# A seventh parked weight slot in five pieces, merged routing products, and conv taps loaded ahead of weight slots

## The chip, the cores and the metric

The kernel runs on one core of one Trainium2 chip. The metric is the device time of one launch in microseconds (us), the median over the runs shown. The core has five engines with queues of their own: TensorE (PE: matmuls; its weight loads are listed as PEld), VectorE (DVE), ScalarE (ACT), GpSimd (POOL) and SyncE (SP, which only issues transfers here). Transfers of all queues share 16 DMA engines. All data are float32.

## What is computed

One layer of a decoder over 288 tokens: 256 of a prompt, and 32 of eight samples. The first half mixes tokens in two branches, the second is a mixture of experts. Cut to what matters:

```python
def layer(x, conv_buf, ...):
    mix, new_buf, v_rows = token_mixers(rmsnorm(x, norm_mix_g), ...)
    x = x + mix
    x = x + moe(rmsnorm(x, norm_ffn_g), ...)

def token_mixers(h, ...):
    u_a, v_a, c_val, c_gate, g_a, g_b = split(h @ w_in)          # w_in: 1024 x 6144
    y_a = (gelu(u_a) * chunk_spatial_mix(layernorm(gelu(v_a)))) @ w_branch_a
    conv = depthwise_conv(concat(conv_buf, c_val * sigmoid(c_gate)), conv_w)   # 31 taps
    y_b = silu(layernorm(conv)) @ w_branch_b + b_branch_b
    merged = sigmoid(g_a + b_gate_a) * y_a + sigmoid(g_b + b_gate_b) * y_b
    return merged @ w_out, new_buf, v_a

def moe(h, ...):                  # 32 experts, each token goes to its best 4
    logits = h @ w_router + b_router
    gates = softmax(top_4(logits))
    # for each expert e, over the tokens x that chose it:
    #   gate, up = split(x @ w_up[e] + b_up[e]);  act = (clip(up) + 1) * gate * sigmoid(1.702 * gate)
    #   y += gates * (act @ w_down[e] + b_down[e])        w_up[e]: 1024 x 2048, w_down[e]: 1024 x 1024
```

The weights of one expert are 12 MB (1 MB is 1,048,576 bytes here): 8 MB of w_up, 4 MB of w_down.

## The kernel before

**The ring.** All large weights go through `ring`, 12 slots of 1 MB (128 partitions of 8 KB). The mixing half fills it three times with 36 blocks (`load_block`, L346). 32 of them are 256 columns of a weight matrix, which lie in the slot as eight runs of 1 KB on each partition; the four of w_out are runs of 4 KB. In the expert half slots 0 to 7 hold w_up of one expert and slots 8 to 11 its w_down, and every partition gets one run of 8 KB (`load_slot`, L383).

**Parked slots.** While expert e is in the ring, the first six slots of w_up of the next expert are loaded into buffers that the mixing half no longer needs (`parked`, L197: two in `big`, one each in R1, R2, R4 and R3). Each of the R buffers has 2304 columns, of which a slot takes 2048. GpSimd copies a parked slot into the ring in four copies of 512 columns (L530) once it has landed (`parked_full`) and the ring slot has been read for the last time (`released`). Slots 6 and 7 of w_up are loaded into the ring directly.

**SyncE's order** is what paces the transfers, since SyncE waits in order. For each of the 30 experts in the loop of L435 it does this: `release_parked` waits for the use of slots 0 to 5 by the last item of the expert before; `load_up_rest` waits for slots 6 and 7 and loads them; `load_parked_again` loads parked slots 0 and 1 of the next expert, once they have been copied out; `load_down` waits for each of the four w_down slots of the expert before, and loads it; then parked slots 2 to 5 follow. The waits are on `up_used` and `down_used`, which TensorE counts up.

**Items.** An expert is worked on in items of 32 tokens; here there are 52 items for 32 experts. TensorE's loop body (from L1428) does the w_up products of the next item (`up`, L1371, eight slots) between the w_down products of the present one (`down`, L1381, four slots), after gathering, turning and combining rows. Experts are put in an order by their counts, computed in the kernel (L962 to L983), with those of one and of two items spread over the list.

**Start.** SyncE loads x, then weight blocks 0 to 3, then the conv cache, the conv taps (`cw_rows`, 31 partitions), b_up and w_spatial, then blocks 4 to 7 (L353 to L367). TensorE works on blocks 0 and 1 first, then turns cache, taps, b_up and w_spatial (L1086, called from L1184 to L1203), and only then blocks 2 and 3. The convolution on VectorE (L800, 240 instructions) needs all of these.

**Mixing.** TensorE does 32 projections of 8 matmuls each in `kind` 0 to 3 (v, u, gate a, gate b); ScalarE evacuates each, with four PSUM banks in turn: projection n waits for the evacuation of n - 4. At projection 18 (`kind` 2, `c` 2) ScalarE also takes the roots of the variances of v, for which it waits on VectorE (`v_stats`, L599).

**Routing.** After the mixing TensorE counts ranks of tokens and counts of experts with products by triangular matrices and by ones (L1338 to L1353). `keep_busy(n)` (L1104) issues n matmuls of 32 columns whose result nobody reads. SyncE loads the w_down slots of the first expert as w_out has been used (L432), and the sixth parked slot behind them, and then waits for `before_known` (L434).

The lines that set the order around the change:

```python
            for k in range(PARKED - 1):
                load_parked(1, k)
            for k in range(UP_SLOTS, SLOTS):
                sp.wait_ge(*mix_block_used(MIX_BLOCKS - SLOTS + k))
                load_slot(0, k)
            load_parked(1, PARKED - 1)
...
                release_parked(before)
                load_up_rest(here, before)
                load_parked_again(place + 1, after, range(0, 2))
                load_down(here, before)
                load_parked_again(place + 1, after, range(2, PARKED))
```

## Time and profile before

| | |
|---|---|
| median of 3 runs | 1298.35 us (1297.46 to 1301.08) |
| the profiled execution's own time | 1300.47 us |
| its span, first to last instruction | 1298.5 us |
| mean granted TensorE clock | 0.97 |
| PE busy | 1182.5 us, 91% of the span |
| PEld busy | 583.8 us, 45% |
| DVE busy | 605.0 us, 47% |
| POOL busy | 467.2 us, 36% |
| ACT busy | 249.5 us, 19% |
| moved by DMA | 448.97 MB (millions of bytes), mean 346 GB/s |

The shares are means over the whole span, and matmuls are pipelined, so a busy PE is not PE at its peak. The stages have different limits: the mixing half and the routing take the first 341 us or so, the experts the rest. The time of the profiled execution differs from its span by 1.97 us, which lie outside the first and the last instruction.

### The profile page before, as it was taken

The page shows a single profiled execution, that of the slowest core. Times are in us where ns is not written, and L with a number is a line of the kernel's source. Part 1 is how long each engine was busy: PE and PEld are TensorE (multiplying, and loading weights), DVE is VectorE, ACT ScalarE, POOL GpSimd, SP SyncE. Part 2 cuts the span into 40 slices and gives each one's busy share as a digit, 9 for nine tenths or more (in the row PEclk, how much of TensorE's full clock was granted, in tenths as well). Part 3 has the DMA queues.
Part 4 walks back from the last instruction along what each step waited for, and adds up shares of the span by engine and source line. Part 5 has one row for each costly group of instructions (what it writes and reads, how often), then busy time and mean ns, then how long its engine had stood idle before and what let it go on. Part 6 is the DMA issues. An engine that isn't in the chain of part 4 may idle for free.

```text
span 1298.5 us, 30625 instructions
## 1 busy us (share of the span) xinstructions
PE 1182.5 (91%) x11129; PEld 583.8 (45%) x11130; DVE 605.0 (47%) x1256; ACT 249.5 (19%) x487; POOL 467.2 (36%) x833
## 2 busy tenths in 40 slices
PE   8999999999999899899778998989989799899876
PEld 6777777775544233333233442333433233333232
DVE  2999984121444344444342444443534244344243
ACT  2012124001122122122121221221211122122112
POOL 1012300000444444435452445454544444535452
PEclk9999999999799999999999999999999999999997
DMA  9983433244699999999999699999999999999996
GB/s 260 339 260 106 142 118 134 100 142 184 244 391 390 422 421 420 422 421 421 421 421 421 252 405 420 422 421 421 422 420 421 421 421 422 421 421 422 421 421 253
DMA packets 94570, 448.97 MB, mean 346 GB/s; under 512 B 8526, under 2 KB 42894, under 8 KB 45339
## 3 DMA queue, kind: packets, MB, share of 16 engines
q1 hardware_dynamic: 93742, 446.55, 85.8%
q10 hardware_dynamic: 749, 1.19, 0.3%
q0 software_dynamic: 48, 0.85, 0.2%
q8 instruction: 15, 0.25, 0.1%
q14 instruction: 16, 0.13, 0.0%
HBM read 447.00 MB, written 2.42 MB: 346 GB/s over the span
## 4 chain that ended last, share of the span: by engine, by line
PE 55%; DMA 16%; DVE 12%; POOL 6%; issue 6%; SPq 4%; ACT 0%; DVEq 0%; POOLq 0%; ACTq 0%
PE banks L1371 20%; DMA ring<-in_w_down 15%; PE banks L1381 12%; DVE R L800 8%; PE banks L1164 8%; POOL ring L530 6%; PE banks L1086 4%; PE banks L1144 3%; PE banks L1123 3%; PE banks L1280 2%; PE banks L1130 1%; SPq L398 1%; DMA R<-in_conv_w 1%; PE banks L1153 1%; SPq L344 1%
## 5 line engine op out<-in xcount | busy, mean ns | idle before, releaser
L1371 PE MATMUL banks<-ring,hT 128*32 128x512 f32 x3328 | 431.6, 612 | 62.3 <-POOL ring L530 57.4
L530 POOL COPY ring<-big 128x512 f32<-128x512 f32 x248 | 146.9, 640 | 564.5 <-SPq L404 564.5
L530 POOL COPY ring<-R 128x512 f32<-128x512 f32 x496 | 289.8, 630 | 111.9 <-DMA R<-in_w_up 111.9
L321 DVE TENSOR_TENSOR xt<-xt,banks 128x1024 f32<-128x1024 f32 x106 | 128.7, 1215 | 401.2 <-PE banks L1144 401.2
L1381 PE MATMUL banks<-ring,hT 128*32 128x256 f32 x3328 | 226.2, 391 | 18.4 <-DMA ring<-in_w_down 13.1
L1381 PEld LDWEIGHTS banks<-ring,hT 128*32 128x32 f32 x3328 | 107.1, 113 | 201.1 <-issue 121.2
L1164 PE MATMUL banks<-hT,ring 128*128 128x288 f32 x768 | 192.0, 411 | 2.5 <-ACT R L602 2.2
L1371 PEld LDWEIGHTS banks<-ring,hT 128*32 128x32 f32 x3328 | 95.5, 111 | 197.5 <-POOL ring L530 81.7
L1164 PEld LDWEIGHTS banks<-hT,ring 128*128 128x128 f32 x768 | 147.2, 193 | 43.5 <-ACT R L602 2.6
L680 ACT COPY WT<-banks 128x256 f32<-128x256 f32 x52 | 19.4, 373 | 495.2 <-PE banks L1381 495.2
L800 DVE SCALAR_TENSOR_TENSOR R<-big,convw,R 128x256 f32<-128x256 f32 x240 | 108.1, 529 | 0.0
L1023 DVE TENSOR_TENSOR hT<-banks,bupT 128x512 f32<-128x512 f32 x52 | 36.0, 692 | 138.5 <-PE banks L1086 138.5
L1144 PE MATMUL banks<-WT 32*128 32x256 f32 x848 | 76.0, 429 | 0.7 <-ACT WT L680 0.7
L1123 PE MATMUL banks<-stage,WT 128*32 128x256 f32 x832 | 56.5, 389 | 17.4 <-issue 17.4
L688 ACT ACT_TABLE_LOAD x51 | 65.4, 1283 | 1.4 <-issue 0.5
L1164 PE MATMUL banks<-R,ring 128*128 128x288 f32 x256 | 62.3, 406 | 0.0
L768 DVE TENSOR_SCALAR WT<-slot_ids,prod 128x128 f32 x153 | 60.2, 448 | 0.0
L1144 PEld LDWEIGHTS banks<-WT 32*128 32x128 f32 x848 | 33.5, 184 | 53.5 <-issue 53.3
L759 DVE TENSOR_SCALAR WT<-slot_ids,prod 128x32 f32 x156 | 55.0, 411 | 0.0
L1123 PEld LDWEIGHTS banks<-stage,WT 128*32 128x32 f32 x832 | 22.6, 110 | 71.7 <-issue 63.5
L1164 PEld LDWEIGHTS banks<-R,ring 128*128 128x128 f32 x256 | 48.6, 190 | 13.4
L1086 PE MATMUL banks<-ident,hT 128*128 128x128 f32 x312 | 52.5, 304 | 0.7 <-ACT hT L670 0.7
(254 smaller groups left out, 766.3 us busy)
## 6 DMA issues: line engine op xcount, KB each, us to landing
ring<-in_w_down SPq DMA_DIRECT2D x128, 1024.0 KB, 11.0
R<-in_w_up SPq DMA_DIRECT2D x124, 1024.0 KB, 18.1
ring<-in_w_up SPq DMA_DIRECT2D x70, 1024.0 KB, 9.4
big<-in_w_up SPq DMA_DIRECT2D x62, 1024.0 KB, 12.8
ring<-in_w_in SPq DMA_DIRECT2D x24, 1024.0 KB, 10.3
ring<-in_w_branch_b SPq DMA_DIRECT2D x4, 1024.0 KB, 5.0
ring<-in_w_branch_a SPq DMA_DIRECT2D x4, 1024.0 KB, 5.0
ring<-in_w_out SPq DMA_DIRECT2D x4, 1024.0 KB, 4.9
```

What stands on the lines that cost most here:

```text
L321: nc.vector.tensor_tensor(dst, dst, rows, ALU.add).then_inc(y_added, 1)
L530: ins = nc.gpsimd.tensor_copy(ring[:, k, h * 512:(h + 1) * 512], parked[k][:, h * 512:(h + 1) * 512])
L688: nc.scalar.activation(ss[:, 15:16], eps_col[:], ACT.Sigmoid)
L759: ins = V.tensor_scalar(sel[:, tt, :], slot_ids[:, bass.ds(rank0, BLK)], rankm[:, tt, bass.ds(expert, 1)], None, ALU.is_equal)
L768: ins = V.tensor_scalar(comb[:, tt], slot_ids[:, bass.ds(rank0, BLK)].unsqueeze(1).to_broadcast([P, QN, BLK]), rankm[:, tt, bass.ds(expert ...
L800: ins = V.scalar_tensor_tensor(acc, cprompt[:, c, k:k + SEQ], convw[:, c, k:k + 1], acc, ALU.mult, ALU.add)
L1086: return nc.tensor.transpose(dst, src, ident[0:n, 0:n])
L1123: mm(XB[q * BLK:(q + 1) * BLK, 0:256], sel[:, tt, :], stage[:, tt, q * 256:(q + 1) * 256], start=tt == 0, stop=False)
L1144: ins = mm(rows[:, q, :], combT[q * BLK:(q + 1) * BLK, tt * P:(tt + 1) * P], out_sb[q * BLK:(q + 1) * BLK, :], start=True, stop=True)
L1164: ins = mm(dst[:, 0:T], w[:, k, h * P:(h + 1) * P], src[:, k, :], start=k == 0, stop=k == KC - 1)
L1371: ins = mm(UP[g * BLK:(g + 1) * BLK, :], xT[:, k, :], ring[:, k, g * 512:(g + 1) * 512], start=k == 0, stop=k == UP_SLOTS - 1)
L1381: ins = mm(DN[q * BLK:(q + 1) * BLK, 0:256], actT[:, f % 4, f // 4, :], ring[:, UP_SLOTS + j, h * D + q * 256:h * D + (q + 1) * 256], star ...
```

## The change

- A seventh slot of w_up is parked. `PARKED` is 7. Five of the whole parked slots keep their buffers; slot 5 is put in five pieces: 768 columns in `stage`, 512 in `tmpc`, and 256 columns at the ends of R1, R2 and R4; R3 now holds slot 6. It is loaded by five transfers (runs of 3, 2, 1, 1 and 1 KB on each partition) and copied by five GpSimd copies. Only slot 7 of w_up is still loaded directly into the ring.
- SyncE waits for `v_stored` before it parks the first slots.
- At the start, weight blocks 2 and 3 are loaded behind cache, taps, b_up and w_spatial.
- ScalarE takes the roots of v at `c` 4 rather than `c` 2.
- The products of the ranks of the sample rows and of the counts share matmuls of 64 columns. Those that need only the first two masks are issued ahead of the wait for the third, where `keep_busy(2)` stood.
- `keep_busy` uses matmuls of 256 columns, and its four other calls have n = 2 for 3.

```diff
-PARKED = 6
+PARKED = 7
...
-        parked = (big[:, 0:SLOT], big[:, SLOT:2 * SLOT], R1[:, 0:SLOT], R2[:, 0:SLOT], R4[:, 0:SLOT], R3[:, 0:SLOT])
+        parked = (big[:, 0:SLOT], big[:, SLOT:2 * SLOT], R1[:, 0:SLOT], R2[:, 0:SLOT], R4[:, 0:SLOT], None, R3[:, 0:SLOT])
+        scattered = (stage[:, 2, 256:1024], tmpc[:].rearrange("p h t -> p (h t)")[:, 0:512], R1[:, SLOT:SLOT + 256],
+                     R2[:, SLOT:SLOT + 256], R4[:, SLOT:SLOT + 256])
+
+        def parked_pieces(k):
+
+            if parked[k] is not None:
+                return [(parked[k][:, h * 512:(h + 1) * 512], h * 512, 512) for h in range(4)]
+            starts = (0, 768, 1280, 1536, 1792)
+            return [(s, lo, s.shape[1]) for s, lo in zip(scattered, starts)]
...
-            for n in range(4):
+            for n in range(2):
                 load_block(n)
...
-            for n in range(4, 8):
+            for n in range(2, 8):
                 load_block(n)
...
-                sp.dma_start(parked[k], src).then_inc(parked_full[k], 16)
+                if parked[k] is not None:
+                    sp.dma_start(parked[k], src).then_inc(parked_full[k], 16)
+                else:
+                    for dst, lo, n in parked_pieces(k):
+                        sp.dma_start(dst, src[:, lo:lo + n]).then_inc(parked_full[k], 16)
...
             sp.wait_ge(ya_evac, 2 * KC)
+            sp.wait_ge(v_stored, 16)
...
-                    pool.wait_ge(parked_full[k], 16 * e)
+                    pool.wait_ge(parked_full[k], 16 * e * (1 if parked[k] is not None else len(scattered)))
                     pool.wait_ge(released, (e - 1) * PARKED + k + 1)
-                    for h in range(4):
-                        ins = nc.gpsimd.tensor_copy(ring[:, k, h * 512:(h + 1) * 512], parked[k][:, h * 512:(h + 1) * 512])
+                    for piece, lo, n in parked_pieces(k):
+                        ins = nc.gpsimd.tensor_copy(ring[:, k, lo:lo + n], piece)
...
-                    if c == 2:
+                    if c == 4:
                         act.wait_ge(v_stats, 1)
...
-            counts, count = DN[0:NE, 0:NE], DN[0:NE, NE:NE + 1]
+            counts, count = bank[4][0:NE, 2 * NE:3 * NE], DN[0:NE, 0:1]
...
-                    mm(TB[:, 0:NE], ones[:], below[:, 0:NE], start=True, stop=True)
+                    mm(TB[:, 0:256], ones[:], slot_ids[:, 0:256], start=True, stop=True)
...
-            keep_busy(2)
+            for t2 in range(2):
+                mm(bank[4][:, NE:3 * NE].rearrange("p (r e) -> p r e", r=2), ones[:],
+                   mask[:, t2:t2 + 1, :].to_broadcast([P, 2, NE]), start=t2 == 0, stop=False)
+            for t2 in range(2):
+                mm(DN[0:NE, 0:1], mask[:, t2, :], ones[:, 0:1], start=t2 == 0, stop=False)
             pe.wait_ge(routed, 3)
-            for t2 in range(2):
-                mm(bank[5][:, NE:2 * NE], ones[:], mask[:, t2, :], start=t2 == 0, stop=False)
-            mm(bank[5][:, NE:2 * NE], below_q[:].rearrange("p q t -> p (q t)"), mask[0:NS, 2, :], start=False, stop=False)
-            mm(bank[5][:, NE:2 * NE], same_row[0:NS].rearrange("p q t -> p (q t)"), rankm[0:NS, 2, :],
-               start=False, stop=True).then_inc(rank_ready, 1)
-            for t2 in range(2):
-                mm(DN[:, 0:NE], ones[:], mask[:, t2, :], start=t2 == 0, stop=False)
-            mm(DN[:, 0:NE], ones[0:NS, :], mask[0:NS, 2, :], start=False, stop=True)
-            for t2 in range(2):
-                mm(DN[0:NE, NE:NE + 1], mask[:, t2, :], ones[:, 0:1], start=t2 == 0, stop=False)
-            mm(DN[0:NE, NE:NE + 1], mask[0:NS, 2, :], ones[0:NS, 0:1], start=False, stop=True).then_inc(counted, 1)
+            mm(bank[4][:, NE:2 * NE], below_q[:].rearrange("p q t -> p (q t)"), mask[0:NS, 2, :], start=False, stop=False)
+            mm(bank[4][:, NE:2 * NE], same_row[0:NS].rearrange("p q t -> p (q t)"), rankm[0:NS, 2, :],
+               start=False, stop=False)
+            mm(bank[4][:, 2 * NE:3 * NE], ones[0:NS, :], mask[0:NS, 2, :], start=False, stop=True).then_inc(rank_ready, 1)
+            mm(DN[0:NE, 0:1], mask[0:NS, 2, :], ones[0:NS, 0:1], start=False, stop=True).then_inc(counted, 1)
```

How the change moves instructions is shown at three places. The first is SyncE's loop over experts, from the loads into ring slots of w_up on. Before (rows that wait are marked; the register instructions between them are part of the listing):

```order
45 L409 REGISTER_ALU [waits up_used]
46 L393 ISA [waits up_used]
47 L393 DMA ring<-in_w_up 128x2048
48 L409 REGISTER_ALU
49 L393 ISA [waits up_used]
50 L393 DMA ring<-in_w_up 128x2048
51 L421 ISA
52 L398 ISA [waits slot_full0]
53 L398 DMA big<-in_w_up 128x2048
```

Now:

```order
48 L422 REGISTER_ALU [waits up_used]
49 L402 ISA [waits up_used]
50 L402 DMA ring<-in_w_up 128x2048
51 L434 ISA
52 L408 ISA [waits slot_full0]
53 L408 DMA big<-in_w_up 128x2048
```

One transfer behind a wait on `up_used` is gone from this place. It stands at the end of the loop body, as five transfers, ahead of the one into R3:

```order
74 L411 ISA [waits slot_full5]
75 L411 DMA stage<-in_w_up 128x768
76 L411 ISA
77 L411 DMA tmpc<-in_w_up 128x512
78 L411 ISA
79 L411 DMA R<-in_w_up 128x256
80 L411 ISA
81 L411 DMA R<-in_w_up 128x256
82 L411 ISA
83 L411 DMA R<-in_w_up 128x256
84 L408 ISA [waits slot_full6]
85 L408 DMA R<-in_w_up 128x2048
```

The second is TensorE's queue in the routing, from the second `keep_busy` to the gather of the first rows. Before:

```order
225 L1107 MATMUL banks<-below,ones 128x32 x2
226 L1344 MATMUL banks<-prod,ones 128x32 [waits routed]
227 L1344 MATMUL banks<-prod,ones 128x32
228 L1345 MATMUL banks<-prod,below_q 128x32
229 L1346 MATMUL banks<-prod,same_row 128x32
230 L1349 MATMUL banks<-prod,ones 128x32 x2
231 L1350 MATMUL banks<-prod,ones 128x32
232 L1352 MATMUL banks<-ones,prod 32x1 x2
233 L1353 MATMUL banks<-ones,prod 32x1
234 L1123 MATMUL banks<-stage,WT 32x256 [waits rows_kept,first_selected]
```

Now:

```order
225 L1356 MATMUL banks<-prod,ones 128x64 x2
226 L1359 MATMUL banks<-ones,prod 32x1 x2
227 L1361 MATMUL banks<-prod,below_q 128x32 [waits routed]
228 L1362 MATMUL banks<-prod,same_row 128x32
229 L1364 MATMUL banks<-prod,ones 128x32
230 L1365 MATMUL banks<-ones,prod 32x1
231 L1137 MATMUL banks<-stage,WT 32x256 [waits rows_kept,first_selected]
```

Behind the wait for the third mask there were ten matmuls up to the gather, and there are four.

The third is ScalarE's queue at gate a (`R` is the evacuated projection, `ss` the roots). Before:

```order
50 L602 ACTIVATE R<-banks,cols 128x288 [waits proj] x2
51 L303 ACT_TABLE_LOAD [waits v_stats]
52 L303 ACTIVATE ss<-mv,eps_col 128x2 [waits proj]
53 L303 ACTIVATE ss<-mv,eps_col 32x1
54 L602 ACT_TABLE_LOAD
55 L602 ACTIVATE R<-banks,cols 128x288
```

Now:

```order
50 L616 ACTIVATE R<-banks,cols 128x288 [waits proj] x4
51 L312 ACT_TABLE_LOAD [waits v_stats]
52 L312 ACTIVATE ss<-mv,eps_col 128x2 [waits proj]
53 L312 ACTIVATE ss<-mv,eps_col 32x1
54 L616 ACT_TABLE_LOAD
55 L616 ACTIVATE R<-banks,cols 128x288
```

Two more evacuations stand ahead of the wait for `v_stats`.

## Rows read from the trace of the kernel before

**Rows 1.** The page, part 2: GB/s moved in 40 slices of 32.5 us.
```profile
GB/s 260 339 260 106 142 118 134 100 142 184 244 391 390 422 421 420 422 421 421 421 421 421 252 405 420 422 421 421 422 420 421 421 421 422 421 421 422 421 421 253
```
**Rows 2.** Windows: length, busy us of PE, PEld, DVE, ACT, POOL; clock, DMA share, GB/s.
```profile
308.00:324.00 16.00, 16.00 (x117) 9.02 (x115) 3.44 (x11) 3.58 (x7) 0.00 (x0) 1.00 0.00 1
...
351.00:424.00 73.00, 71.18 (x849) 29.62 (x845) 35.31 (x75) 17.20 (x34) 32.65 (x59) 1.00 0.96 386
424.00:712.00 288.00, 253.32 (x2875) 97.29 (x2867) 114.47 (x227) 56.10 (x108) 127.73 (x216) 0.98 1.01 421
712.00:729.00 17.00, 16.58 (x201) 6.84 (x201) 8.73 (x16) 4.22 (x8) 10.85 (x20) 1.00 0.28 105
729.00:767.00 38.00, 37.57 (x450) 15.72 (x443) 18.67 (x44) 8.46 (x17) 16.22 (x29) 1.00 0.99 403
767.00:1283.00 516.00, 455.64 (x5150) 176.57 (x5146) 212.84 (x414) 99.36 (x193) 241.12 (x408) 0.97 1.01 421
```
**Rows 3.** DMA view, window 62 to 75 us: weight blocks in runs of 1 KB.
```profile
DMA packets 4499, 4.53 MB, mean 348 GB/s; under 512 B 75, under 2 KB 4499, under 8 KB 4499
```
**Rows 4.** DMA view, window 450 to 700 us: expert slots in runs of 8 KB.
```profile
DMA packets 14458, 105.35 MB, mean 421 GB/s; under 512 B 1599, under 2 KB 1599, under 8 KB 1599
```
**Rows 5.** Timeline of SyncE: start, us, what it issued, how many.
```profile
429.13 1.89 SPq L398 DMA_DIRECT2D R<-in_w_up  x4
...
665.53 1.89 SPq L398 DMA_DIRECT2D R<-in_w_up  x4
...
758.28 1.95 SPq L393 DMA_DIRECT2D ring<-in_w_up  x2
...
767.15 5.50 SPq L393 DMA_DIRECT2D ring<-in_w_down  x4
772.83 1.88 SPq L398 DMA_DIRECT2D R<-in_w_up  x4
...
1248.88 1.88 SPq L398 DMA_DIRECT2D R<-in_w_up  x4
```
**Rows 6.** Timeline at the start: start, us, instruction; in brackets idle before and releaser.
```profile
30.67 4.61 PE L1086 MATMUL banks<-ident,R 31*128 31x31 f32 x32 [1.28 <-DMA R<-in_conv_w]
```
**Rows 7.** Timeline at gate a.
```profile
174.65 1.28 ACT L303 ACT_TABLE_LOAD   x1 [14.38 <-DVE mv L839]
...
178.29 21.36 PE L1164 MATMUL banks<-hT,ring 128*128 128x288 f32 x80 [2.18 <-ACT R L602]
...
186.56 2.54 DVE L856 TENSOR_TENSOR R<-R,banks 128x2304 f32<-128x2304 f32 x1
...
191.93 2.12 ACT L607 ACTIVATE big<-R 128x2304 f32<-128x2304 f32 x1 [3.38 <-PE banks L1164]
...
194.08 4.17 DVE L866 TENSOR_REDUCE tmpc<-big 128x288 f32<-128x2304 f32 x1 [3.72 <-ACT big L607]
...
199.49 0.65 PE L1239 MATMUL banks<-tmpc,mean_w 128*128 128x288 f32 x2
```
**Rows 8.** Windows at the start, at gate a and in the routing.
```profile
32.00:39.00 7.00, 7.00 (x30) 5.83 (x30) 5.04 (x14) 0.00 (x0) 0.00 (x0) 0.54 1.07 345
...
179.00:183.00 4.00, 4.00 (x13) 2.88 (x12) 3.93 (x4) 0.42 (x2) 0.00 (x0) 0.65 0.33 113
...
329.00:346.00 17.00, 17.00 (x96) 10.78 (x100) 7.28 (x41) 1.76 (x3) 2.84 (x6) 0.51 0.66 271
```
**Rows 9.** Timeline of PE in the routing.
```profile
334.52 1.94 PE L1123 MATMUL banks<-stage,WT 128*32 128x256 f32 x16
...
338.00 1.49 PE L1107 MATMUL banks<-below,ones 128*128 128x32 f32 x6
...
341.02 5.89 PE L1371 MATMUL banks<-ring,hT 128*32 128x512 f32 x32
```
**Rows 10.** The page, part 5: GpSimd's copies out of the R buffers.
```profile
L530 POOL COPY ring<-R 128x512 f32<-128x512 f32 x496 | 289.8, 630 | 111.9 <-DMA R<-in_w_up 111.9
```

More of the change, by code:

```diff
@@ L957, in _ @@
             dve.wait_ge(rank_ready, 2)
-            link(V.tensor_copy(rankm[:, 2, :], bank[5][:, NE:2 * NE]))
+            link(V.tensor_copy(rankm[:, 2, :], bank[4][:, NE:2 * NE]))
             select_first(2)
@@ L1328, in _ @@
             sum_quarters(bank[0][:, 256:257])
-            keep_busy(3)
+            keep_busy(2)
             pe.wait_ge(h2T_ready, 5)
@@ L1334, in _ @@
             ins.then_inc(logits_ready, 1)
-            keep_busy(3)
+            keep_busy(2)
             pe.wait_ge(routed, 2)
@@ L1362, in _ @@
             mm(bank[6][:, 0:2 * NE], ones[0:NE, :], placed, start=True, stop=True).then_inc(order_summed, 1)
-            keep_busy(3)
+            keep_busy(2)
             turn_rows(0)
-            keep_busy(3)
+            keep_busy(2)
             def up(k, fills):
```

## Prediction

> **What bounds the kernel now.** I read the page's row of GB/s first: from slice 13 on it stands at 420 to 422, but for one dip to 252 in slice 22 [rows 1]. So the expert half is limited by how fast weights arrive, and next I asked the windows where that is so and where not. They give four kinds of stretch [rows 2]:
> - up to 351 us DMA has room. From 308 to 324 us it moves 1 GB/s.
> - 351 to 424 us: 386 GB/s, PE busy 71.18 of 73 us. PE is the bound; DMA stands still now and then because all buffers are full.
> - 424 to 712 us: 421 GB/s, DMA share 1.01, PE busy only 253 of 288 us. DMA is the bound.
> - 712 to 767 us: PE has more to do than data come in (105, then 403 GB/s). PE is the bound. From 767 to 1283 us DMA is the bound again, and a tail of 15.5 us follows.
>
> These stretches stand in series. What PE saves before 351 us moves all that follows; what a transfer costs more in the two DMA-bound stretches (804 us together) is paid in full; in the PE-bound stretches a transfer is hidden.
>
> **Part 1, the pieces.** The slot in five pieces moves the same bytes in more packets. The trace has a price for short runs. Where blocks come in runs of 1 KB, DMA is as busy as it can be and moves 348 GB/s [rows 3]; with runs of 8 KB it moves 421 GB/s [rows 4]. A MB takes 3.013 us in the one case and 2.491 us in the other. On each of 16 engines a MB is 64 runs and one small packet (the 75 under 512 B of 4499) in the first, 8 runs and one small packet (1599 of 14458) in the second. The 56 packets between them cost 0.522 us: 9.3 ns for each packet, whatever its length. A slot in five pieces has 8 partitions x 5 runs = 40 packets on an engine, and 5 small ones at the ends of five transfers, 45 for 9 before. 36 x 9.3 ns = 0.34 us for each expert. I assume that runs of 2 and 3 KB are one packet each; they have no row of their own, and both ends of the price hold for them.
>
> How often is it paid? Once for each expert whose parked group goes out in a DMA-bound stretch and is ahead of data that PE waits for. Such groups run from the one at 429.13 to the one at 665.53 us (nine), and from 772.83 to 1248.88 us (seventeen) [rows 5]. The other four of the loop lie in PE-bound stretches. 26 x 0.34 = **8.7 us more**. At 8 ns a packet it is 7.5, at 11 ns (were the small packets dearer) 10.3.
>
> The Trainium skill (DMA: Bandwidth & Descriptors, Specifications) names 512 bytes as the smallest transfer for line rate; by that, runs of 1 KB would cost nothing. Rows 3 and 4 do not agree: 1 KB runs lose 17% of the rate at full DMA share. Without the price the sum below would be 8.7 us lower, and I keep that as a rival.
>
> GpSimd copies 7 slots for 6. A slot takes it 4 x 0.63 = 2.5 us [rows 10], five copies of the same columns about as long, and it idles for more than half of 424 to 712 us (127.73 us busy of 288) [rows 2]. Where DMA is the bound, slot 6 is copied (2.5 us) while slot 7 lands (2.49 us), so it is in the ring when slot 7 is, and the next wait of PE, that for w_down data, takes up the rest. I cost this at nothing; if the cover went, it would be at most one up product, under 1 us in an item.
>
> **Part 2, the deeper buffer.** One more MB loaded ahead sounds like 2.5 us at the start of each DMA-bound stretch: 5.0 us for both. But look at which wait ends last there. SyncE's order has two gates in each round: the loads of slots 6 and 7 (at 758.28 us in the last round of the PE-bound stretch) and the loads of w_down (767.15 us) [rows 5]. Before, four MB go out between the gates, two up slots and two parked; that is 10.0 us of DMA for 8.9 us between the gates. Afterwards it is three MB, 7.5 us. The MB gained ahead of the first gate is missing behind it: at the w_down gate the same bytes have been issued in both kernels, and what counts from there on is only whether DMA still has a backlog. So the gain is at most the idle time of DMA ahead of the first gate. In 729 to 767 us that is 38 x (421 - 403)/421 = 1.6 us in all, less 0.34 for the pieces, and a part goes to the latency of the first w_down transfer. I take 0.6 us there and as much at the end of the first PE-bound stretch, which has the same pattern, **1.2 us less**; ends 0 and 5.0. The sleeping stretch of 712 to 729 us gets shorter by its beginning, but its end is set by PE. The new parked MB of the first expert goes out in the empty time at 308 to 324 us and costs nothing, and the wait for `v_stored` ended long before.
>
> **Part 3, the start.** PE waits 1.28 us for the taps [rows 6]. Two MB of blocks now go behind them, 6.0 us at 348 GB/s, so the taps are there 4.7 us before PE asks. Blocks 2 and 3 are last of the same bytes, and PE needs block 2 only behind the turns. The 4.61 us of turns end at 35.3 us [rows 6]; VectorE's convolution follows them, so it moves along, and it has to, since PE waits for its sum later on. **1.3 us less**; ends 0 and 3.4 (the clock is at 0.54 for 7 us right there [rows 8], and might not fall).
>
> **Part 4, the roots.** ScalarE waits 14.38 us for `v_stats` with two evacuations behind it, and PE waits 2.18 us for one of them; right after, from 179 to 183 us, the clock is 0.65 [rows 7, 8], 1.4 us lost. With the wait two evacuations later, PE finds its banks free, and the roots still start when VectorE is done at 174.6 us, so VectorE loses nothing. What is late next? The reduction of the squares ends at 194.08 + 4.17 = 198.25 us, for PE's product at 199.49 [rows 7]: 1.2 us of slack. The squares (2.12 us) wait for a projection of PE, which comes earlier, and for the subtraction that ends at 186.56 + 2.54 = 189.10 us; they can start there rather than at 191.93, 2.8 us earlier, and so can the reduction. PE arrives 3.6 us earlier, 0.8 us more than that, out of a slack of 1.2: it just fits. **3.6 us less** (2.2 + 1.4); ends 1.5 and 3.9.
>
> **Part 5, the routing.** Half of ten matmuls behind the third mask are gone or stand ahead of it; the gather starts at 334.52 us now [rows 9] and could start about 1.8 us earlier (ranks come at the same time, the counts follow after one short product rather than six). But two wide `keep_busy` matmuls do the work of 512 columns. A projection is 8 matmuls of 288 columns. Five (80 records, two a matmul) take 21.36 us with 1.4 us lost to the clock [rows 7], so one matmul takes 0.50 us; 256 columns are 0.44 us, and 0.89 at half clock. Two are 1.8 us where three narrow ones took 1.3 to 1.5 (the row at 338.00), and this comes twice ahead of the first up product at 341.02. If the clock stays at half (0.51 from 329 to 346 us [rows 8]) I get 1.8 - 2 x 0.5 = **0.8 us less**. Were the clock full there, the products up to 346 us would gain up to 4 us; were the fillers wholly in the way, 1 us could be lost.
>
> **The sum.** 8.7 - 1.2 - 1.3 - 3.6 - 0.8 = 1.8 us more. On the profiled execution that is 1300.47 + 1.8 = 1302.3 us; on the median of the runs, 1298.35 + 1.8 = **1300.2 us**. A measurement of this kernel can tell about 0.3%, 3.9 us, from no change. So I forecast no difference that can be told, from two amounts of 7 to 9 us against each other.
>
> **Rivals.**
> - *Short runs are free.* Then only the gains are left: 1298.35 - 6.9 = 1291.5 us, faster. For it: the rule cited. Against it: rows 3 and 4. Chance 0.10.
> - *The clock holds and the buffer is worth more.* With wide fillers and without the two waits PE is not slowed at 32, 179 and 329 us: 2.1 us more from the start, 3.2 from the routing, up to 3.8 from the buffer. 1300.2 - 5.3 = 1294.9 us, down to 1291.1. For it: the low clock follows PE's stalls and narrow products. Against it: the long row of turns at the start stays, and PE's work between the fillers stays narrow. Chance 0.20, of which 0.14 falls more than 3.9 us below.
> - *Transfers cost more than packets.* Each of the four more transfers for a slot has a cost of its own on the 16 engines that one long transfer hides. From 0.02 us each (26 x 4 x 0.02 = 2.1 us) the time is past 0.3%; at 0.05 us it is 1300.2 + 5.2 = 1305.4 us, slower. For it: no row shows transfers this short back to back. Against it: 9 packets a MB already fit the rate, so a transfer's end costs little. Chance 0.18.
> - *The gains of parts 3 and 4 are taken back by VectorE* (its convolution and reductions become what PE waits for): 1300.2 + 4.0 = 1304.2 us. The slack of 1.2 us in part 4 is thin. Chance 0.05.
> - The forecast: 0.47.
>
> **Numbers.** Faster: 0.10 + 0.14 = 0.24. Slower: two thirds of 0.18, the 0.05, and 0.03 of the forecast's own spread, 0.20. Same: 0.56. The range takes in the lower case with the clock in its greater part and the price of transfers at its 0.05 us: 1292 to 1306 us.
>
> **What would show it.** In the trace of the changed kernel: 421 GB/s in the DMA-bound stretches should fall to about 421 x 29.9/30.2 = 416 (an expert's 12 MB take 12 x 2.491 = 29.9 us), with the time of one expert up by 0.34 us; PE should have no wait at the taps nor behind ScalarE near 178 us; the first up product should start near 341.0 - 5.7 = 335.3 us; the dip should still be there, its PE-bound end unmoved against PE's own work. I am wrong if the rate stays at 421 (pieces free), if it falls below 413 (transfers dear), or if the first up product starts before 332 or after 338 us.

## The result, and the profile after

| | before | after |
|---|---|---|
| median of the runs | 1298.96 us (4 runs, 1297.46 to 1301.08) | 1373.72 us (4 runs, 1371.45 to 1376.95) |
| profiled execution, its span | 1298.5 us | 1373.8 us |
| granted clock, mean | 0.970 | 0.943 |

The ratio is 1.058, 95% interval 1.0553 to 1.0600: the changed kernel is 74.8 us slower. The median before is that of the three runs of the prediction and a fourth. Forecast were 1300.2 us and a range that ended at 1306. No rival reached this far, and none named the place where the time went.

The page of the changed kernel, part 2 (GB/s in 40 slices of 34.3 us), and part 5, two groups of VectorE and GpSimd (busy us, mean ns | idle before, releaser):
```profile
GB/s 267 338 238 115 139 123 98 151 249 181 384 355 363 418 354 390 386 366 384 369 408 286 357 385 376 364 370 373 376 407 364 411 371 370 416 347 376 416 352 279
...
L544 POOL COPY ring<-R 128x512 f32<-128x512 f32 (+1 forms) x589 | 311.7, 578 | 0.1
...
L1040 DVE TENSOR_SCALAR hT<-hT 128x256 f32<-128x256 f32 x52 | 103.9, 1999 | 1.8
```
The flat row of 421 GB/s of [rows 1] is gone, so DMA is no longer the bound throughout. GpSimd, which waited 111.9 us for data [rows 10], waits 0.1 us ahead of these copies. And one instruction of VectorE, the first clamp in `activate` (L1026 before, L1040 now), takes 2.0 us in the mean. The same group before, from the view by groups:
```profile
L1026 DVE TENSOR_SCALAR hT<-hT 128x256 f32<-128x256 f32 x52 | 21.1, 405 | 1.8
```
The view of one tile's instructions gives each line's shortest, median and longest in ns. After:
```profile
L1037 DVE TENSOR_TENSOR hT<-banks,bupT x52: 690/692/693, 344.8 to 1355.5; 128x512 f32<-128x512 f32 x52
L1040 DVE TENSOR_SCALAR hT<-hT x52: 293/295/8210, 345.5 to 1356.2; 128x256 f32<-128x256 f32 x52
```
The median is unchanged at 295 ns. The long instances are nine of 7.5 to 8.2 us and ten of 2.4 us. The bias add, which reads PSUM (`banks`), never takes longer, and nor does L790, which reads PSUM too (405/417/423 ns). Waits of PE, after (us in total, times, longest):
```profile
PE banks L1383 <- DVE hT L790: 86.4, 20, 7.8
```
L790 is the product that hands PE the next item's columns; VectorE issues it right behind the clamp, and it is short itself. So PE waits for an instruction that stands behind a held one. Before, the same wait was 3.1 us in total. What holds the clamp shows in one timeline of all engines (start, us, instruction, in brackets the idle time before), of which these are the rows of VectorE, GpSimd and PE around one instance:
```profile
463.97 4.51 POOL L544 COPY ring<-big 128x512 f32<-128x512 f32 x8 [14.19 <-SPq L417]
...
468.42 6.73 POOL L544 COPY ring<-R 128x512 f32<-128x512 f32 x12
...
471.26 0.69 DVE L1037 TENSOR_TENSOR hT<-banks,bupT 128x512 f32<-128x512 f32 x1 [2.51 <-PE banks L1100]
...
471.98 7.88 DVE L1040 TENSOR_SCALAR hT<-hT 128x256 f32<-128x256 f32 x1
...
475.09 0.82 POOL L544 COPY ring<-stage 128x768 f32<-128x768 f32 x1
475.86 0.61 POOL L544 COPY ring<-tmpc 128x512 f32<-128x512 f32 x1
476.41 3.31 POOL L544 COPY ring<-R 128x256 f32<-128x256 f32 x7
479.79 0.41 DVE L790 TENSOR_TENSOR hT<-banks,cols 128x256 f32<-128x256 f32 x1
...
480.43 3.64 PE L1383 MATMUL banks<-ring,hT 128*32 128x512 f32 x16 [7.48 <-DVE hT L790]
```
GpSimd's copies of the seven slots run from 463.97 to 479.72 us without a gap. The bias add, whose source is in PSUM, passes in the middle of them. The clamp, from SBUF to SBUF, starts at 471.98 and ends at 479.86, when the last copy is done. Before, such a row of six slots ended just in time (GpSimd, then VectorE, of the kernel before):
```profile
749.66 4.61 POOL L530 COPY ring<-big 128x512 f32<-128x512 f32 x8 [17.97 <-SPq L404]
754.21 8.98 POOL L530 COPY ring<-R 128x512 f32<-128x512 f32 x16
```
```profile
762.54 0.69 DVE L1023 TENSOR_TENSOR hT<-banks,bupT 128x512 f32<-128x512 f32 x1 [2.55 <-PE banks L1086]
763.27 0.29 DVE L1026 TENSOR_SCALAR hT<-hT 128x256 f32<-128x256 f32 x1
```
The row ends at 763.19 us and the clamp comes at 763.27. A slot more is 2.2 to 2.5 us more of copies, and there were 0.08 us of slack.

A row without a gap doesn't hold everything, though. At its beginning VectorE's SBUF-to-SBUF instructions get in (GpSimd, then VectorE, after):
```profile
363.96 4.59 POOL L544 COPY ring<-big 128x512 f32<-128x512 f32 x8 [13.45 <-SPq L417]
```
```profile
363.84 1.45 DVE L782 TENSOR_SCALAR WT<-slot_ids,prod 128x128 f32 x3
365.21 1.71 DVE L773 TENSOR_SCALAR WT<-slot_ids,prod 128x32 f32 x3
...
377.59 2.36 DVE L1040 TENSOR_SCALAR hT<-hT 128x256 f32<-128x256 f32 x1
```
The six `tensor_scalar` of L782 and L773 pass one by one between the first copies. Those that meet a copy take 0.59 to 0.65 us each, where the shortest of these lines take 0.33 and 0.23. The clamp of the same row, 13.6 us in, is held until the row ends at 379.79 us. In the kernel before, a clamp 1.8 us into a row passes too:
```profile
433.50 5.02 POOL L530 COPY ring<-big 128x512 f32<-128x512 f32 x8 [14.03 <-SPq L404]
```
```profile
435.33 0.60 DVE L1026 TENSOR_SCALAR hT<-hT 128x256 f32<-128x256 f32 x1
```
In all 13 kernels with a trace here, none of some 3100 instances of VectorE's SBUF-to-SBUF lines that came behind fewer than 13 copies of a row without a gap took more than 0.64 us over its line's shortest. All holds of over 1 us came behind 13 copies or more. That is where the holds stand, not why: no run varied the number of copies alone.

Windows of after, columns as in [rows 2]: 354 and 385 GB/s where [rows 2] have 386 and 421, and PE is busy 240 us of 288 where it was 253.
```profile
351.00:424.00 73.00, 68.18 (x780) 27.67 (x776) 33.81 (x61) 14.30 (x28) 31.68 (x58) 0.95 0.90 354
424.00:712.00 288.00, 240.45 (x2622) 90.44 (x2614) 126.21 (x210) 51.24 (x100) 141.89 (x260) 0.91 0.96 385
```
Ahead of the experts all went better than forecast. Windows and PE's timeline of after, which answer to [rows 6 to 9]:
```profile
27.00:39.00 12.00, 12.00 (x78) 10.29 (x77) 7.37 (x21) 0.41 (x1) 0.00 (x0) 1.00 1.08 350
160.00:200.00 40.00, 38.49 (x159) 29.34 (x158) 31.89 (x43) 9.33 (x14) 0.12 (x1) 1.00 0.38 127
310.00:342.00 32.00, 30.39 (x297) 17.69 (x295) 17.53 (x72) 8.08 (x16) 8.02 (x14) 1.00 0.46 186
```
```profile
195.51 0.75 PE L1253 MATMUL banks<-tmpc,mean_w 128*128 128x288 f32 x2 [1.43 <-DVE tmpc L880]
...
330.21 0.43 PE L1374 MATMUL banks<-prod,ones 32*128 32x64 f32 x2 [1.15 <-DVE prod L990]
...
332.72 1.50 PE L1383 MATMUL banks<-ring,hT 128*32 128x512 f32 x12
```
The clock is 1.00 in all three places, the waits for the taps and for ScalarE are gone, and the first up product starts at 332.72 instead of 341.02 us, 8.3 us earlier for 5.7 forecast. So the loss is larger than 74.8: some 83 us between 333 us and the end.

### The profile page after: what moved, and what is told of

It reads as the page before. It is cut to its first block, busy times and chain, and to the rows that moved or that the text cites. A ratio compares the mean times of both kernels' runs of the same rounds, so it can differ in the third digit from the quotient of the medians.

```text
span 1373.8 us, 31173 instructions
## 1 busy us (share of the span) xinstructions
PE 1198.8 (87%) x11113; PEld 581.3 (42%) x11114; DVE 669.8 (49%) x1256; ACT 248.1 (18%) x487; POOL 523.4 (38%) x988
## 4 chain that ended last, share of the span: by engine, by line
PE 53%; DVE 21%; DMA 11%; SPq 5%; POOL 5%; issue 4%; ACT 1%; DVEq 0%; POOLq 0%; ACTq 0%
PE banks L1383 21%; PE banks L1393 12%; DMA ring<-in_w_down 11%; DVE R L814 8%; PE banks L1178 7%; DVE hT L1040 7%; POOL ring L544 5%; PE banks L1100 3%; PE banks L1137 2%; PE banks L1158 2%; PE banks L1294 2%; SPq L408 2%; SPq L411 2%; PE banks L1144 1%; DVE hT L1037 1%
## 5 line engine op out<-in xcount | busy, mean ns | idle before, releaser
L1383 PE MATMUL banks<-ring,hT 128*32 128x512 f32 x3328 | 462.1, 650 | 141.1 <-DVE hT L790 86.4
L544 POOL COPY ring<-big 128x512 f32<-128x512 f32 x248 | 143.2, 625 | 698.1 <-SPq L417 698.1
L544 POOL COPY ring<-R 128x512 f32<-128x512 f32 (+1 forms) x589 | 311.7, 578 | 0.1
L1383 PEld LDWEIGHTS banks<-ring,hT 128*32 128x32 f32 x3328 | 97.3, 115 | 291.7 <-issue 170.3
L1393 PEld LDWEIGHTS banks<-ring,hT 128*32 128x32 f32 x3328 | 109.7, 115 | 192.9 <-issue 138.3
L1040 DVE TENSOR_SCALAR hT<-hT 128x256 f32<-128x256 f32 x52 | 103.9, 1999 | 1.8
L782 DVE TENSOR_SCALAR WT<-slot_ids,prod 128x128 f32 x153 | 55.9, 421 | 0.0
L773 DVE TENSOR_SCALAR WT<-slot_ids,prod 128x32 f32 x156 | 53.5, 402 | 0.0
L689 ACT ACTIVATE hT<-hT 128x256 f32<-128x256 f32 x52 | 21.7, 417 | 172.5 <-DVE hT L1040 172.5
## 6 DMA issues: line engine op xcount, KB each, us to landing
R<-in_w_up SPq DMA_DIRECT2D x124, 1024.0 KB, 15.7
ring<-in_w_up SPq DMA_DIRECT2D x39, 1024.0 KB, 10.5
```

The source lines that it names most:

```text
L544: ins = nc.gpsimd.tensor_copy(ring[:, k, lo:lo + n], piece)
L773: ins = V.tensor_scalar(sel[:, tt, :], slot_ids[:, bass.ds(rank0, BLK)], rankm[:, tt, bass.ds(expert, 1)], None, ALU.is_equal)
L782: ins = V.tensor_scalar(comb[:, tt], slot_ids[:, bass.ds(rank0, BLK)].unsqueeze(1).to_broadcast([P, QN, BLK]), rankm[:, tt, bass.ds(expert ...
L1040: V.tensor_scalar(lin3[:, :, 0:64], lin3[:, :, 0:64], LIMIT, None, ALU.min).then_inc(g1_ready, 1)
L1383: ins = mm(UP[g * BLK:(g + 1) * BLK, :], xT[:, k, :], ring[:, k, g * 512:(g + 1) * 512], start=k == 0, stop=k == UP_SLOTS - 1)
L1393: ins = mm(DN[q * BLK:(q + 1) * BLK, 0:256], actT[:, f % 4, f // 4, :], ring[:, UP_SLOTS + j, h * D + q * 256:h * D + (q + 1) * 256], star ...
```

## The experiments

Two theories at first. **Hold:** a gap-free row of GpSimd's copies keeps an SBUF-to-SBUF instruction of VectorE that comes late in it out until it ends. **SyncE:** SyncE is held up while it issues the five small transfers, releases the slots late, and that late release is the loss. The second has a row in the timeline of SyncE, after:
```profile
452.61 6.71 SPq L411 DMA_DIRECT2D R<-in_w_up  x3
459.50 1.99 SPq L408 DMA_DIRECT2D R<-in_w_up  x1
```
Three small transfers take 6.71 us to issue here and 1.37 us at 493.51 us (I take it that DMA has a backlog in the first place and none in the second), and the row of copies above starts late, at 463.97.

**Another form of the clamp.** Both clamps as `scalar_tensor_tensor`.
```diff
-  V.tensor_scalar(lin3[:, :, 0:64], lin3[:, :, 0:64], LIMIT, None, ALU.min)
+  V.scalar_tensor_tensor(lin3[:, :, 0:64], lin3[:, :, 0:64], LIMIT, lin3[:, :, 0:64], ALU.min, ALU.min)
```


> The changed kernel with one edit: the two clamps of the activation (one after the bias add, one after it on the other half) are written as scalar_tensor_tensor with a second operand rather than as tensor_scalar. Nothing else moves. Theory A (VectorE's clamp cannot run while GpSimd copies without a pause, and is held until the row of copies ends; it took 1999 ns on average for 405 before): the form with a second operand is not held, the wait of PE for VectorE behind it (86.4 us) goes, and the time falls by 65 to 85 us to 1290 to 1308. Theory B (the five small transfers keep SyncE and so the ring late, and VectorE's long clamp is a symptom that costs nothing): no change, 1374. Theory C (GpSimd is the bound, its copies take longer than an item): 1360 or more, and PE waits for GpSimd instead.

Measured: 1371.13 us, ratio 1.055 (1.0534 to 1.0569). The view by groups, then VectorE's timeline:
```profile
L1042 DVE SCALAR_TENSOR_TENSOR hT<-hT 128x256 f32<-128x256 f32 x52 | 103.0, 1980 | 1.8
```
```profile
469.08 7.69 DVE L1042 SCALAR_TENSOR_TENSOR hT<-hT 128x256 f32<-128x256 f32 x1
...
668.03 0.43 DVE L1042 SCALAR_TENSOR_TENSOR hT<-hT 128x256 f32<-128x256 f32 x1
```
A miss for the theory in that form. The first clamp alone is shown; the second was changed likewise, with a constant tile for its lower limit. Both forms are held alike, so neither the operation nor one input or two makes the difference. One instance got away: the clamp at 668.03 us stands 7.7 us into a row that began at 660.35 and takes 0.43 us, where others at the same place were held for 8 us. What decides at that point is open.

**Six parked slots**, with the other edits as they are.
```diff
-PARKED = 7
+PARKED = 6
-  parked = (..., R4[:, 0:SLOT], None, R3[:, 0:SLOT])
+  parked = (..., R4[:, 0:SLOT], R3[:, 0:SLOT])
```


> The changed kernel with six whole parked slots as before, and all its other edits (taps first, roots later, merged products, wide fillers, the added wait). All theories: the slowdown goes. What the other edits are worth: the first up product started 8.3 us earlier in the changed kernel's trace (332.72 for 341.02), so 1299.0 - 8.3 = 1290.7 us; if something of it is given back in the transfer-bound stretches, up to 1299.

Measured: 1290.77 us, ratio 0.993 (0.9917 to 0.9950), 8.8 us below the kernel before. The whole loss comes with the seventh slot; the other edits gain more than forecast.

**More copies, no transfers.** The kernel before, with slot 5's data copied once more into buffers that nothing uses then.
```diff
-  for h in range(4):
+  for h in list(range(4)) * (2 if k == PARKED - 1 else 1):
...
```


> The kernel before with one edit: behind slot 5 GpSimd makes five more copies (768, 512, 256, 256, 256 columns, from the parked slot into unused buffer ends) ahead of its signal. No transfer is added, and no slot. Theory A: the row of copies grows from 13.4 to 15.6 us, longer than the 13.6 us from the release to the next clamp; the clamp is held by about 2.1 us in each expert where the data are all there (some 20 of 31), so its mean rises above 1 us and the time by 20 to 50 us where PE is the bound and less where transfers are; 1310 to 1350. Theory B: no added transfers, so 1299 to 1303 (slot 5 is 2.2 us late).

Measured: 1311.61 us, ratio 1.010 (1.0082 to 1.0116). GpSimd's and VectorE's timeline at one of the four places where the clamp is held:
```profile
726.22 8.95 POOL L530 COPY ring<-R 128x512 f32<-128x512 f32 x16
735.12 0.82 POOL L535 COPY stage<-R 128x768 f32<-128x768 f32 x1
...
736.44 1.08 POOL L535 COPY R<-R 128x256 f32<-128x256 f32 x3
```
```profile
735.30 2.37 DVE L1032 TENSOR_SCALAR hT<-hT 128x256 f32<-128x256 f32 x1
```
The hold comes without a byte or a transfer more, and ends at 737.67 us where the row of copies does (737.52). It stays rare: four times for some 20 expected, all in the PE-bound stretches, where all data are there. The four are 2.4 us each, some 8 us over the usual clamp, of the 12.0 us that this kernel is slower. In the DMA-bound ones GpSimd still waited for data, 79.4 us in all, and the gaps let VectorE in.

**A slot in pieces, but six slots.** The seventh slot out, the sixth scattered.
```diff
-  parked = (..., R4[:, 0:SLOT], None, R3[:, 0:SLOT])
+  parked = (..., R4[:, 0:SLOT], None)
```


> The changed kernel with six parked slots, the sixth in the five pieces (R3 unused), all other edits kept. Against the run with six whole slots only the shape of one slot differs: five transfers for one, five copies for four. The prediction's price of 9.3 ns a packet gives 26 x 0.34 = 8.7 us more than that run. Theory A: the row of copies is only 0.1 to 0.2 us longer than with six whole slots, so the clamp is not held and nothing else is added. Theory B (small transfers block SyncE and make the releases late): 30 us or more above the run with six whole slots.

Measured: 1296.69 us, ratio 0.998 (0.9965 to 0.9986), 5.9 us over six whole slots. Window 767 to 1280 us:
```profile
767.00:1280.00 513.00, 451.32 (x5050) 173.77 (x5054) 198.32 (x413) 97.91 (x190) 237.84 (x425) 0.96 1.02 417
```
This is the price of the pieces by itself, five copies for four included. From the first up product to the end of the span it is 963.2 us here and 956.8 us with six whole slots, 6.4 us more. The clamp is not held (its longest is 757 ns).

**The seventh slot with a gap in GpSimd's row.** This tells the two theories apart: the copies, the transfers and SyncE's program are those of the changed kernel, and GpSimd only waits behind each slot for its own last copy.
```diff
                     ins.then_inc(slot_full[k], 16)
+                    pool.wait_ge(slot_full[k], 16 * (FILLS + 1) + 16 * e)
```


> The changed kernel, with GpSimd waiting behind each slot until its own last copy is complete (one wait on its own semaphore, so that a row of copies has a short gap every 2.5 us). Nothing else is changed: same copies, same transfers, same release by SyncE. Theory G (VectorE's clamp is kept out by a gap-free row of GpSimd copies until the row ends): the clamp gets in at the next slot boundary, so no hold above about 2.6 us; the mean of the clamp falls from 2.0 us to under 1.0, PE's waits for VectorE's act product from 86 us to under 25, and the time comes to 1300 to 1325 us. Rival S (SyncE, blocked for 6 to 9 us behind the five small transfers, releases the slots late, and that is what costs the time; the held clamp only shows it): the row of copies starts as late as before, and the time stays above 1355 us.

Measured: 1298.77 us (10 runs), ratio 1.000 (0.9989 to 1.0013). One wait for each slot takes off 75 us. Tile view, GpSimd's timeline and SyncE's, then a row of GpSimd and one of VectorE from the round after SyncE's, of this kernel:
```profile
L1041 DVE TENSOR_SCALAR hT<-hT x52: 293/295/559, 346.4 to 1279.0; 128x256 f32<-128x256 f32 x52
```
```profile
774.78 4.62 POOL L544 COPY ring<-big 128x512 f32<-128x512 f32 x8 [14.39 <-SPq L417]
779.47 6.97 POOL L544 COPY ring<-R 128x512 f32<-128x512 f32 x12
786.50 0.83 POOL L544 COPY ring<-stage 128x768 f32<-128x768 f32 x1
...
787.82 3.43 POOL L544 COPY ring<-R 128x256 f32<-128x256 f32 x7
```
```profile
448.25 6.35 SPq L411 DMA_DIRECT2D R<-in_w_up  x3
454.78 1.99 SPq L408 DMA_DIRECT2D R<-in_w_up  x1
```
```profile
459.28 4.63 POOL L544 COPY ring<-big 128x512 f32<-128x512 f32 x8 [13.51 <-SPq L417]
...
467.84 0.34 DVE L1041 TENSOR_SCALAR hT<-hT 128x256 f32<-128x256 f32 x1
```
The clamp's longest instance falls from 8210 to 559 ns, though the row is as full as before but for gaps too short to be listed as idle time (779.40 to 779.47 us is one). SyncE is held up as long as in the changed kernel (6.35 and 1.99 us), and it costs nothing that shows. The theory of SyncE falls. Behind the first row, the clamps that meet a row still come 8 us and more into it (467.84 us in the one from 459.28), but never more than three copies behind a gap. The time also lies below the 1300 to 1325 us that I expected. I expected a held clamp to wait for the next gap, up to 2.6 us; instead it gets in between two copies of a slot, as at the beginning of a row. Nothing of the hold is left.

**A gap behind every copy.** As above, with a wait behind each of the 29 copies of a row.
```diff
                     for piece, lo, n in parked_pieces(k):
+                        if lo:
+                            done += 1
+                            ins.then_inc(copied, 1)
+                            pool.wait_ge(copied, done)
                         ins = nc.gpsimd.tensor_copy(ring[:, k, lo:lo + n], piece)
```


> As the kernel before this one, but GpSimd waits behind every single copy (a gap every 0.6 us). Theory G: a hold is at most one copy, 0.8 us; the clamp's mean falls to about 0.5 us, PE's waits for VectorE to under 5 us, and what is left of the change is the pieces: 1290.8 (six slots and the other edits) + 5.9 (the price of a slot in pieces, measured) = 1296.7 us, less up to 2 for the deeper buffer, plus up to 5 for slower copies: 1294 to 1302 us. Rival S: above 1355 us. Rival C (the row of copies is longer with seven slots and gates PE itself): PE would wait for slots rather than for VectorE, 1310 to 1340 us.

Measured: 1318.96 us, ratio 1.017 (1.0145 to 1.0192). A miss upward. The hold is gone here too, but part 4 of the page (the chain that ended last) names the copies:
```profile
PE banks L1390 22%; POOL ring L550 15%; PE banks L1400 11%; DVE R L821 8%; PE banks L1185 8%; PE banks L1107 5%; PE banks L1165 4%; PE banks L1144 3%; SPq L409 2%; PE banks L1301 2%; SPq L412 2%; PE banks L1151 2%; PE banks L1174 2%; DVE R L830 1%; DVE R L833 0%
```
POOL has 15% of the chain, against 3% with a wait per slot and 5% in the changed kernel. A row of seven slots takes 19.9 us (579.37 to 599.30), 15.7 without waits (463.97 to 479.72). That is 4.2 us for 29 waits, 0.14 us each with whatever VectorE now takes from a copy. PE waits 90.9 us for the copies, against 81.4 with a wait per slot and 54.5 in the changed kernel. Rival C of its expectation comes true here: the copies themselves become what PE waits for.

**Six slots with a gap behind every copy.** The same edit on the kernel with six whole slots.

> Six whole parked slots and the other edits (1290.8 us), with GpSimd waiting behind every copy. Theory G: with six slots the clamp was held only once or twice for 2 us, so there is little to win: 1289 to 1292 us. If the extra waits make the copies slower enough to matter, 1292 to 1297 us.

Measured: 1289.19 us, ratio 0.993 (0.9912 to 0.9945), as expected. With 24 copies for 29 the waits cost nothing that shows; against 1290.77 us without them it is no difference that these runs can tell.

**The other parts, each alone on the kernel before.** The taps ahead of two more blocks; the roots behind c = 4; the merged products with the old fillers; the wide fillers with the old products.
```diff
-            for n in range(4):
+            for n in range(2):
...
-            for n in range(4, 8):
+            for n in range(2, 8):
```


> The kernel before with one edit: four taps loads behind weight blocks 0 and 1 rather than behind 0 to 3. Forecast's term: -1.3 us, ends 0 and -3.4. The first up product (at 341.02 us before) starts 0 to 3.4 us earlier. My reading of the traces of before and after is that the clock stays at 1.00 from 27 to 39 us, so I now expect -2.5 to -3.5 there, if VectorE's convolution (unmoved in the changed kernel, at 36.5 us) doesn't take it back; if it does, 0.

```diff
-                    if c == 2:
+                    if c == 4:
```


> The kernel before with one edit: ScalarE takes the roots behind the evacuations of c = 4 rather than c = 2. Forecast's term: -3.6 us, ends -1.5 and -3.9. The granted clock from 179 to 183 us should rise from 0.65 to 1.00.

The third has the change's edits between the second mask and the gather alone.

> The kernel before with the merged rank and count products alone, the fillers of TensorE narrow as before. Forecast's term for the routing was -0.8 us in all, of which the merge is -1.8. If the full clock in the changed kernel (1.00 for 0.51 from 310 to 342 us) comes from the merge, the first up product starts 3 to 4 us earlier; if it comes from the wide fillers, 1 to 2 us.

```diff
-                    mm(TB[:, 0:NE], ones[:], below[:, 0:NE], start=True, stop=True)
+                    mm(TB[:, 0:256], ones[:], slot_ids[:, 0:256], start=True, stop=True)
...
-            keep_busy(3)
+            keep_busy(2)
```


> The kernel before with the wide fillers alone (two of 256 columns for three narrow ones). Forecast's term: +1.0 us if the clock stays at half, and a gain of up to 4 us less that if it stays full. If the full clock comes from the wide fillers, it shows here: granted clock above 0.9 from 329 to 346 us and a first up product 1 to 3 us earlier.

| part alone | median us (before: 1299.39) | ratio, 95% interval | gain, us | forecast, us |
|---|---|---|---|---|
| taps | 1298.21 | 0.9990 (0.9980 to 1.0001) | 1.2 | 1.3 |
| roots | 1297.06 | 0.9980 (0.9971 to 0.9990) | 2.3 | 3.6 |
| merge | 1297.68 | 0.9984 (0.9973 to 0.9996) | 1.7 | 1.8 |
| wide fillers | 1294.10 | 0.9958 (0.9943 to 0.9973) | 5.3 | -1.0 |

The four add up to 10.5 us where together they give 8.8. Each gain is known to 1.2 to 2 us either way, so that is no difference these runs can tell, and the interval of the taps takes in no change.

For where a gain arises there is one traced execution of each kernel, and these differ in places that no edit touched: from 32 to 39 us the clock was 0.54 before [rows 8] and 1.00 in the kernel with the wide fillers alone, whose fillers come 280 us later. So I read stretches, not the first up product alone.

The taps alone bring PE to gate a earlier, and the wait there grows from 2.18 us [rows 7] to 3.60, so that the first up product starts at 341.28 us, no earlier than before.
```profile
178.33 22.38 PE L1164 MATMUL banks<-hT,ring 128*128 128x288 f32 x80 [3.60 <-ACT R L602]
```
VectorE's convolution starts at 36.61 us (36.52 before), so what ScalarE waits for is no earlier. That explains a small gain alone; that the taps count once the roots have moved is likely, but no run has just these two. The roots alone do what was forecast: PE runs through gate a without a wait, in the timeline of that kernel,
```profile
171.67 22.47 PE L1164 MATMUL banks<-hT,ring 128*128 128x288 f32 x92
194.16 0.75 PE L1239 MATMUL banks<-tmpc,mean_w 128*128 128x288 f32 x2
```
and its clock from 179 to 183 us is 1.00. The second row stood at 199.49 us [rows 7], 5.3 us later; this execution was the fastest of its ten, and the medians give 2.3 us. The largest part is the fillers. Alone they bring the first up product to 335.87 us, 5.2 us earlier, the merge alone to 338.22 us, 2.8 us earlier. Of the 5.2 us, 1.9 stand already at 199.49 us (197.64 there). From PE's product in `sum_quarters`, just ahead of the first fillers, to the first up product it is 14.8 us before, 11.5 with the wide fillers and 12.3 with the merge. The window 329 to 346 us, with the wide fillers alone, then with the merge alone:
```profile
329.00:346.00 17.00, 15.57 (x163) 7.47 (x166) 11.85 (x42) 3.01 (x6) 8.86 (x16) 1.00 0.64 250
```
```profile
329.00:346.00 17.00, 17.00 (x113) 8.81 (x117) 8.60 (x44) 1.41 (x3) 5.65 (x11) 0.60 0.64 264
```
Against 0.51 before [rows 8] the clock is 1.00 with wide fillers and 0.60 with the merge: the fillers, not the merge, keep it up.

## Why the prediction was wrong

- **The step that failed** is the last paragraph of part 1: "GpSimd copies 7 slots for 6 ... it idles for more than half of 424 to 712 us ... I cost this at nothing". It ends with the bound "under 1 us in an item". The cover I named was idle time, and that it exists is true. I asked only who waits for the copies, not who can't run beside them. Where all data are there the copies come in a row without a gap; that row was 13.5 us long, and the next clamp came 13.6 us behind its start. One slot more reached into the clamp, and in the changed kernel nearly every row is without a gap. In place of nothing the runs show 74.8 us, the difference of the changed kernel (+74.8 us to before) and the same with a gap per slot (0.0): the clamp waits for the end of the row, up to 8.2 us, and PE behind it 86.4 us in all. My own sign would have misled me: the rate from 424 to 712 us fell to 385 GB/s, which I had marked as "transfers dear" (below 413), while the pieces without the hold run at 417.
- **That the slack could have been seen.** The two rows of the kernel before at 763.19 and 763.27 us stand in its trace, and so do clamps of up to 778 ns for a median of 295. I looked at neither, since VectorE was busy less than half the time. They show that the two engines collide and that there was no slack; how long a hold lasts when a row is longer, no clamp of that trace shows. The Trainium skill (SBUF — State Buffer, Who interferes with whom) says that "only the shared port pair causes contention, and it's an exclusive lock", between VectorE and GpSimd. The trace agrees as to these two: ScalarE's activation from SBUF to SBUF in the same items takes 416 to 418 ns throughout. It agrees also that VectorE's instruction waits for the other engine to be done, since the held clamps of the changed kernel end some 0.15 us behind the last copy. The runs show more: behind 13 copies and more without a gap the hold spans the whole rest of the row rather than one copy.
- **Part 1, the pieces:** the mechanism holds, the size was off: 5.9 us measured for 8.7. The page's slices with the pieces stand at 417 to 418 GB/s for 421; on 29.9 us for an expert that is 0.25 us for 0.34 forecast, some 6 to 7 ns a packet for 9.3. Both rivals on the pieces fall: they are not free, and transfers cost no more than I had reckoned for their packets.
- **Part 2, the deeper buffer:** forecast -1.2 us. With the hold taken away, seven slots (0.0 us to before) stand 2.9 us above six with one in pieces (-2.9) by the medians. In the traces both take the same from the first up product to the end of the span, 963.1 us (333.58 to 1296.7) and 963.2 (331.95 to 1295.1). No gain shows, and no loss in the expert half either. The runs don't part the waits from what the buffer itself gives; that stays open.
- **Parts 3 and 4:** both waits went as forecast. By size, 1.2 us for 1.3 (not told from nothing) and 2.3 for 3.6. Together with part 5 they bring 8.8 us for 5.7 forecast. The slack of 1.2 us in part 4 was spent as feared, but only 1.43 us of a new wait came of it.
- **Part 5** was wrong in its sign for the fillers: +1.0 forecast with the clock at half, -5.3 measured with the clock at full (by the medians; in the trace, 3.3 us lie between the mixing and the first up product). I had the price for it ("Were the clock full there, the products up to 346 us would gain up to 4 us") and took the other side.
- **The sum without the hold:** -8.8 + 5.9 + 2.9 = 0.0 us, the 1298.8 us of the run with a gap per slot. It closes because the 2.9 us are what was left over, not a measured term. That it lies 0.1% from the forecast is luck and no sign that the terms were right: parts 3 to 5 were 3.1 us better, the pieces 2.8 us cheaper, and the rest 4.1 us worse (+2.9 for -1.2) than their terms.
- **Why 75 us and not 12.** With more copies and no transfers, the same amount of copying cost 12 us (1311.6 to 1299.6). There data are late in the DMA-bound stretches and gaps come by themselves; with the seventh slot GpSimd waits 0.1 us for data in the whole run, so nearly every row is without a gap. The nine long holds make three quarters of the held time. They stand in rows that start late behind SyncE's small transfers, so that the clamp comes 8 us into the row rather than 13.6: that is where SyncE's delay counts, as a multiplier of the hold and not by itself. This reading rests on the timelines; no run took SyncE's delay away alone.

The version to keep is six whole slots with the other edits: 1290.8 us, 1289.2 with a gap per copy, 0.7% under the kernel before. With seven slots, one wait for each slot takes the loss away, but gains nothing on six.

## What to carry to other kernels

Before a copy is given to GpSimd "because it idles", look at which SBUF-to-SBUF instructions of VectorE fall into its row of copies and how far the row's end is from the next one; slack is counted there, not in busy shares. Compare the longest with the median of each line in the trace: a line whose longest is a multiple of its median may already collide somewhere. A wait of GpSimd on its own last result, once every 2 us or so, opened the row here at the cost of 0.1 to 0.2 us each; behind every short copy of a row that PE waits for, such waits made the row itself a bound (+20 us).

## What the hardware did that I had not expected

- GpSimd's copies, back to back, kept one instruction of VectorE out for up to 8.2 us, over more than ten copies, but only where 13 copies or more lay behind it in the row; earlier ones got in after one copy. A gap of some 0.07 us behind each slot (779.40 to 779.47 us above) was enough to end the holds. Both `tensor_scalar` and `scalar_tensor_tensor` from SBUF to SBUF were held (1999 and 1980 ns in the mean); the additions and products out of PSUM in the same rows never were (690/692/693 ns).
- SyncE took 2.0 to 2.4 us to issue each small transfer at 452.61 us and 0.46 us at 493.51 us (6.71 and 1.37 us for three).
- Two matmuls of 256 columns in place of three of 32 held the granted clock at 1.00 instead of 0.51 over 17 us; the kernel with them alone was 5.3 us faster.
